# Adding the shift of the rows on one engine, the sigmoid ahead of the rows, and the first row loads on another queue

## The chip, the cores and the metric

The kernel runs on one core of a Trainium2 chip. TensorE (PE), VectorE (DVE), ScalarE (ACT), GpSimd (POOL) and SyncE (SP) each run an instruction stream of their own and meet through semaphores; SP, ACT and POOL can also issue transfers, each on a queue of its own, and 16 DMA engines carry them. The metric is the time of one execution on the device in microseconds (us). Lower is better.

## What is computed

Two layers (DEPTH = 2) over 256 latent tokens and 256 context tokens of width 1024; the second layer processes only the 256 latent tokens. Each layer has a block of token mixers and then a mixture of 16 experts with grouped routing. The part that matters here is the second:

```python
hx2 = modulate(rms_norm(x, g_norm2[l]), sh2, sc2)      # h * (1 + scale) + shift
...
s = jax.nn.sigmoid((t @ w_router).astype(F32))
sel = s + b_router.astype(F32)
grp_score = jnp.sum(lax.top_k(grp, TOP_K)[0], axis=-1)  # best of 4 groups
_, eidx = lax.top_k(jnp.where(emask, sel, -jnp.inf), TOP_K)   # 2 experts inside it
...
for e in range(N_EXPERTS):
    y = (jax.nn.silu(t @ w_gate[e]) * (t @ w_up[e])) @ w_down[e]
    out = out + combine[:, e:e + 1] * y
```

All tensors are float32. The weights of one expert are 6 MB, so each layer reads 96 MB of them.

## The kernel before

**Routing.** When a layer's mixers are done, PE transposes the normalised activations into rows of tokens (`rows`, one bank for each half row of 512 columns of a tile of 128 tokens; four tiles in layer 0, two in layer 1). ACT evicts each half with the token's norm as a factor into `trow` (`rows_out_`, semaphore `row_a`). The modulation's shift is still missing in these rows; it is added to `trow` from `shift_b`, a copy of the shift on all partitions, one for each sequence. The order of the tiles is that of `row_tile`: 2, 3, 0, 1 in layer 0 and 0, 1 in layer 1. POOL adds it to all tiles but tile 1, half by half (L742), DVE to tile 1 (L1234 in the trace, the line of a helper that records every `tensor_tensor`; other helpers' lines are L1237, L1240 and, for ACT, L774).

ACT also takes the sigmoid of the router's logits (`rt`), behind its first two evictions. From it DVE makes the routing in some 40 small instructions (`grp`, `rt`, `tokv`), ending in `routed`; PE makes from its masks the place of each token in its expert (`places`, L2332 to L2334).

**Steps.** Experts are ranked by their number of tokens. An order written out by hand (`ORDER`) runs 27 steps in layer 0 and 18 in layer 1; a step is one expert with up to 64 of its tokens (`C`; some have 32). The experts 0 and 1 (`LEADERS`) come first in both layers, with weights that are loaded ahead. Weights lie in two slots of six units of 1 MB (`wexp`), and SP issues a unit when the step that last used its place has freed it (`used`), in an order fixed by the plan. In a step PE does: gate and up (L2393), the transposes of the next step's rows (L1962), the down product of the step before (L2408), and the turn of this step's result (L1962 or L2442). In layer 1 the weighted results are also added up on PE (`combine`, L2426).

**How rows reach a step.** The first four steps of layer 0 and the first two of layer 1 (`PICKED`) pick their rows from `trow` by a product with a 0/1 matrix `pick` that DVE makes (L2377, `step_rows`). All later steps load theirs from DRAM: POOL writes `trow` with indirect transfers to `x_rows` in the experts' order (`rowid` gives the place; L752, semaphore `scattered`; eight in layer 0, four in layer 1), and the rows of a step are then loaded to `xpick` (four places, `XR`). The first three row loads of a layer are issued by SP (L562) in the midst of its weights, ahead of expert 10 in layer 0 and of expert 6 in layer 1 (`ROWS_AHEAD`), after a wait for `scattered`; the others by ACT (L1086), one for each step. The transposes of a loaded step's rows stand in PE's order ahead of the down product of the step before.

Of the kernel before, what the change touches and what calls it, by code (L numbers as in the profile page):

```python
# [10 lines left out]
ROWS_AHEAD = (10, 6)  # L11
# [149 lines left out]
def hybrid_backbone(nc, A, out):  # L161
# [139 lines left out]
    with ctx:  # L301
# [159 lines left out]
        shift_b = [at_byte("shift_b0", [P, D], f32, CONV), at_byte("shift_b1", [P, D], f32, R6)]  # L461
# [78 lines left out]
        def span(l):  # L540

            return TOK if l < DEPTH - 1 else SEQ

        def seqs(l):
            return span(l) // SEQ

# [13 lines left out]
        def _(sp):  # L560
# [3 lines left out]
            for l in range(DEPTH):  # L564
# [70 lines left out]
                for r, j in plan.issue(plan.loads[LEADERS[l]:], 4, EC):  # L635
                    if (r, j) == (ROWS_AHEAD[l], 0):

                        sp.wait_ge(sem("all", "scattered"), sum(2 * (span(i) // P) for i in range(l + 1)) * 16)
                        for i in range(XR - 1):
                            row, w = plan.steps[PICKED[l] + i][3:]  # L640
                            load(l, f"xload{i}", xpick[0:w, i, :], x_rows[l][row:row + w, :])
# [41 lines left out]
        def _(pool):  # L683
# [5 lines left out]
            for l in range(DEPTH):  # L689
# [43 lines left out]
                NT = T // P  # L733
                pool.wait_ge(sem("all", "x_back2"), back2(l))
                for t in [row_tile(l, b)[0] for b in range(NT)]:
                    if t == 1:
                        continue
                    for c in range(2):
                        b = [row_tile(l, b) for b in range(2 * NT)].index((t, c))
                        pool.wait_ge(S("row_a"), b + 1)  # L740
                        h = slice(c * 512, (c + 1) * 512)
                        ins = nc.gpsimd.tensor_tensor(trow[:, t, h], trow[:, t, h], shift_b[t // 2][:, h], ADD)  # L742
                        if c == 0:
                            p.step(ins)
                    ins.then_inc(S("hm"), 1)
                p.sync()
                pool.wait_ge(S("hm"), 2 * KT + NT - 1)
                pool.wait_ge(S("h2"), seqs(l) * KT + 1)
                pool.wait_ge(S("rowid_ok"), 1)
                for t in range(T // P):  # L750
                    for c in range(2):
# [3 lines left out]
                        ).then_inc(sem("all", "scattered"), 16)  # L755

# [15 lines left out]
        def _(act):  # L772
# [6 lines left out]
            for l in range(DEPTH):  # L779
# [289 lines left out]
                for b in range(2):  # L1069
                    rows_out_(b)  # L1070
                act.wait_ge(S("lgT"), 3)
                fn(rt[:, 0, 0:NT * NE], rt[:, 0, 0:NT * NE], ACT.Sigmoid).then_inc(S("affin"), 1)
                for b in range(2, 2 * NT):
                    rows_out_(b)
# [112 lines left out]
                def scale_first(t):  # L1187

                    act.wait_ge(sem("all", f"yg{t}"), (l + 1) * 2 * 16)
# [39 lines left out]
        def _(dve):  # L1229
# [15 lines left out]
            for l in range(DEPTH):  # L1245
# [461 lines left out]
                for c in range(2):  # L1707
# [4 lines left out]
                    if c == 0:  # L1712
                        v.step(ins)
# [863 lines left out]
```

## Time and profile before

| | us |
|---|---|
| median of 3 runs | 1424.6 |
| lowest, highest | 1423.45, 1424.93 |
| the profiled execution, its own time | 1430.6 |
| its span | 1428.8 |
| PE busy | 1252.2 (88%) |
| DVE busy | 627.1 (44%) |
| ACT busy | 366.2 (26%) |
| POOL busy | 131.5 (9%) |

The rows come from one profiled execution. Its page cuts the span into 40 slices of 35.7 us and gives each engine's busy share in tenths. Other views give single instructions in order of time, with the idle time ahead of them and who ended it, or the busy time of all engines in a chosen stretch. A float32 product appears as two PE instructions.

### The profile page before, as it was taken

The numbers are of one execution on the slowest core, as the hardware profiler recorded it, in microseconds if no ns is written. First come the engines' busy times: TensorE is split into PE (matmuls) and PEld (weight loads), VectorE is DVE, ScalarE is ACT, GpSimd is POOL, SyncE is SP. The second block draws the span as 40 slices with busy tenths as digits, with TensorE's granted clock in tenths as the row PEclk, the third lists the DMA queues.
The fourth block names the chain that finished last, engine by engine and source line by source line (L and its number), as shares of the span: only waits on it lengthen the run. The fifth ranks groups of instructions, "written<-read, shape, count | busy, mean of one in ns | idle before, by whom it ended". The sixth has DMA issues, their size and how long they took to land.

```text
span 1428.8 us, 20033 instructions
## 1 busy us (share of the span) xinstructions
PE 1252.2 (88%) x8172; PEld 794.8 (56%) x8172; DVE 627.1 (44%) x1124; ACT 366.2 (26%) x595; POOL 131.5 (9%) x121
## 2 busy tenths in 40 slices
PE   3699897899999787999999957987899978898986
PEld 1477576787787632334343326775789843343443
DVE  2627448685546442122131126575776661221222
ACT  2632125334243300000100014523454520000000
POOL 0000000000004220000000020004940210000000
PEclk9899999999999989999999987998999989999998
DMA  9747894232224469699899983866264579999996
GB/s 382 283 187 318 362 395 165 89 89 89 89 89 151 198 260 349 249 360 349 330 353 398 415 325 116 324 265 220 105 136 161 193 291 363 389 395 399 396 420 267
DMA packets 59887, 382.71 MB, mean 268 GB/s; under 512 B 8913, under 2 KB 11413, under 8 KB 20309
## 3 DMA queue, kind: packets, MB, share of 16 engines
q1 hardware_dynamic: 45968, 346.18, 62.5%
q10 hardware_dynamic: 9748, 18.74, 4.0%
q0 software_dynamic: 4080, 16.53, 3.2%
q8 instruction: 64, 1.05, 0.3%
q14 instruction: 27, 0.21, 0.0%
HBM read 363.84 MB, written 44.84 MB: 286 GB/s over the span
## 4 chain that ended last, share of the span: by engine, by line
issue 24%; PE 22%; DMA 9%; DVE 7%; ACT 2%; POOL 2%; SPq 0%; POOLq 0%; DVEq 0%; ACTq 0%
DMA wexp<-in_expert 7%; PE bank L2408 3%; PE bank L1995 3%; PE bank L1996 3%; PE bank L1997 3%; PE bank L2393 3%; PE bank L1962 2%; PE bank L2426 1%; DMA x_rows<-trow,rowid 1%; DVE wlo L1234 1%; POOL x_rows L752 1%; DVE rt L1234 1%; DMA stage<-in_in 1%; POOL m_lo L721 1%; PE bank L2274 1%
## 5 line engine op out<-in xcount | busy, mean ns | idle before, releaser
L2393 PE MATMUL bank<-wexp,xg 128*64 128x512 f32 (+1 forms) x1504 | 265.5, 596 | 12.0 <-DMA wexp<-in_expert 9.0
L1995 PE MATMUL bank<-h_hi,whi 128*128 128x512 f32 (+1 forms) x640 | 226.1, 353 | 23.0 <-DVE wlo L1234 13.8
L1996 PE MATMUL bank<-h_lo,whi 128*128 128x512 f32 (+1 forms) x640 | 220.5, 345 | 0.0
L1997 PE MATMUL bank<-h_hi,wlo 128*128 128x512 f32 (+1 forms) x640 | 220.3, 344 | 0.0
L2393 PEld LDWEIGHTS bank<-wexp,xg 128*64 128x64 f32 (+1 forms) x1504 | 77.8, 125 | 164.2 <-issue 144.7
L2408 PE MATMUL bank<-wexp,act_a 128*32 128x256 f32 (+1 forms) x1072 | 151.9, 504 | 16.9 <-DMA wexp<-in_expert 13.9
L1234 DVE TENSOR_TENSOR wlo<-stage,whi 128x2048 fp32r<-128x2048 f32 x56 | 133.3, 2387 | 68.8 <-ACT whi L774 67.1
L1995 PEld LDWEIGHTS bank<-h_hi,whi 128*128 128x128 f32 x640 | 125.1, 195 | 47.8 <-DVE wlo L1234 18.7
L774 ACT ACTIVATE whi<-stage 128x2048 fp32r<-128x2048 f32 x56 | 106.9, 1910 | 101.2 <-DMA stage<-in_in 59.6
L1996 PEld LDWEIGHTS bank<-h_lo,whi 128*128 128x128 f32 x640 | 124.7, 195 | 13.6 <-issue 0.5
L1997 PEld LDWEIGHTS bank<-h_hi,wlo 128*128 128x128 f32 x640 | 124.4, 194 | 13.8
L1234 DVE TENSOR_TENSOR act_a<-act_s,bank 128x256 f32<-128x256 f32 (+1 forms) x47 | 17.1, 364 | 254.8 <-ACT act_s L774 254.8
L774 ACT ACTIVATE yrow<-bank 128x512 f32<-128x512 f32 (+1 forms) x40 | 20.7, 517 | 348.7 <-PE bank L2408 273.4
L1839 DVE COPY gu_sb<-bank 128x512 f32<-128x512 f32 x47 | 32.5, 691 | 166.7 <-PE bank L2393 166.6
L2408 PEld LDWEIGHTS bank<-wexp,act_a 128*32 128x32 f32 (+1 forms) x1072 | 51.0, 129 | 89.8 <-issue 68.5
L1240 DVE SCALAR_TENSOR_TENSOR conv<-glu,vec,conv 128x512 f32<-128x512 f32 (+1 forms) x90 | 57.5, 679 | 1.0 <-DVE amp L1234 0.3
L1962 PEld LDWEIGHTS bank<-tables,xpick 32*128 32x128 f32 (+1 forms) x328 | 24.1, 142 | 46.2 <-issue 31.4
L1995 PE MATMUL bank<-m_hi,whi 128*128 128x512 f32 (+1 forms) x128 | 44.3, 346 | 4.2 <-POOL m_lo L721 4.1
L1996 PE MATMUL bank<-m_lo,whi 128*128 128x512 f32 (+1 forms) x128 | 43.8, 342 | 0.0
L1997 PE MATMUL bank<-m_hi,wlo 128*128 128x512 f32 (+1 forms) x128 | 43.7, 341 | 0.0
L1240 DVE SCALAR_TENSOR_TENSOR xT<-bank,modT,xT 128x256 f32<-128x256 f32 (+1 forms) x64 | 22.7, 409 | 45.4 <-PE bank L1997 38.0
L721 POOL TENSOR_TENSOR m_lo<-merged,m_hi 128x512 fp32r<-128x512 f32 (+1 forms) x16 | 24.1, 1539 | 194.1 <-ACT m_hi L774 194.1
(340 smaller groups left out, 1641.2 us busy)
## 6 DMA issues: line engine op xcount, KB each, us to landing
wexp<-in_expert SPq DMA_DIRECT2D x192, 1024.0 KB, 15.4
stage<-in_in SPq DMA_DIRECT2D x40, 1024.0 KB, 8.5
raw<-in_mod SPq DMA_DIRECT2D x18, 1024.0 KB, 8.2
stage<-in_mod SPq DMA_DIRECT2D x16, 1024.0 KB, 5.0
x_rows<-in_c_zero SPq DMA_DIRECT2D x32, 512.0 KB, 11.1
y_rows<-in_c_zero SPq DMA_DIRECT2D x20, 512.0 KB, 12.0
spare<-in_mod SPq DMA_DIRECT2D x8, 1024.0 KB, 13.7
stage<-in_out SPq DMA_DIRECT2D x8, 1024.0 KB, 4.7
```

Of the source, the lines that this page charges most:

```text
L721: nc.gpsimd.tensor_tensor(m_lo[:, t, 0:T], merged[:, t, 0:T], m_hi[:, t, 0:T].bitcast(f32), SUB).then_inc(S("m_lo"), 1)
L752: pool.indirect_dma_start(out=x_rows[l], out_offset=bass.IndirectOffsetOnAxis(ap=rowid[:, 2 * t + c:2 * t + c + 1], axis=0), in_=trow[:, t ...
L774: return nc.scalar.activation(out_, in_, f, **kw)
L1234: return V.tensor_tensor(o, x, y, op)
L1240: return V.scalar_tensor_tensor(out=o, in0=x, scalar=s, in1=y, op0=op0, op1=op1)
L1839: V.tensor_copy(gu_sb[:, :], bank[0][:, :]).then_inc(S("gu_sb"), 1)
L1962: return nc.tensor.transpose(o, i, ident[0:n, 0:n])
L1995: MM(o, w[0], x_[0], start=start, stop=False)
L1996: MM(o, w[0], x_[1], start=False, stop=False)
L1997: return MM(o, w[1], x_[0], start=False, stop=stop)
L2393: ins = MM(bank[0][g * w:(g + 1) * w, :], x_[:, 2 * j + k, :], wexp[:, z, j, c], start=(first_ == 0), stop=(last_ == 0))
L2408: ins = MM(bank[3][h * w:(h + 1) * w, 0:8 * w], a_[:, kk, :], wexp[:, z, 4 + j, c], start=(kk == 0), stop=(kk == 3))
```

## The change

The shift is added by DVE alone, a whole tile of 1024 columns at a time: the first tile once the routing is done, the others behind the picks of the leading experts. PE's first picked step takes the tiles in the order in which they come and waits for each. POOL's additions and their waits go, and `shift_b1` moves to another place in memory. ACT takes the sigmoid before any eviction. The first three row loads of both layers are issued by POOL, right behind its scatter, and SP no longer waits for the scatter. The semaphores of the rows are counted accordingly.

```diff
-ROWS_AHEAD = (10, 6)
...
-        shift_b = [at_byte("shift_b0", [P, D], f32, CONV), at_byte("shift_b1", [P, D], f32, R6)]
+        shift_b = [at_byte("shift_b0", [P, D], f32, CONV), at_byte("shift_b1", [P, D], f32, RK)]
...
+        def row_loads(r):
+
+            return (r // XR + (1 if r % XR == XR - 1 else 0)) * 16
...
                 for r, j in plan.issue(plan.loads[LEADERS[l]:], 4, EC):
-                    if (r, j) == (ROWS_AHEAD[l], 0):
-
-                        sp.wait_ge(sem("all", "scattered"), sum(2 * (span(i) // P) for i in range(l + 1)) * 16)
-                        for i in range(XR - 1):
-                            row, w = plan.steps[PICKED[l] + i][3:]
-                            load(l, f"xload{i}", xpick[0:w, i, :], x_rows[l][row:row + w, :])
...
-                NT = T // P
-                pool.wait_ge(sem("all", "x_back2"), back2(l))
-                for t in [row_tile(l, b)[0] for b in range(NT)]:
-                    if t == 1:
-                        continue
-                    for c in range(2):
-                        b = [row_tile(l, b) for b in range(2 * NT)].index((t, c))
-                        pool.wait_ge(S("row_a"), b + 1)
-                        h = slice(c * 512, (c + 1) * 512)
-                        ins = nc.gpsimd.tensor_tensor(trow[:, t, h], trow[:, t, h], shift_b[t // 2][:, h], ADD)
-                        if c == 0:
-                            p.step(ins)
-                    ins.then_inc(S("hm"), 1)
-                p.sync()
-                pool.wait_ge(S("hm"), 2 * KT + NT - 1)
-                pool.wait_ge(S("h2"), seqs(l) * KT + 1)
+                pool.wait_ge(S("h2"), seqs(l) * KT + T // P)
                 pool.wait_ge(S("rowid_ok"), 1)
...
+                pool.wait_ge(sem("all", "scattered"), sum(2 * (span(i) // P) for i in range(l + 1)) * 16)
+                for i in range(XR - 1):
+                    row, w = plans[l].steps[PICKED[l] + i][3:]
+                    load("all", f"yg{i}", xpick[0:w, i, :], x_rows[l][row:row + w, :])
...
                 act.wait_ge(S("hn"), (KT if l == 0 else 2 * KT) + 1)
-                for b in range(2):
-                    rows_out_(b)
                 act.wait_ge(S("lgT"), 3)
                 fn(rt[:, 0, 0:NT * NE], rt[:, 0, 0:NT * NE], ACT.Sigmoid).then_inc(S("affin"), 1)
-                for b in range(2, 2 * NT):
+                for b in range(2 * NT):
                     rows_out_(b)
...
                 ins.then_inc(S("routed"), 1)
-                for c in range(2):
-
-                    dve.wait_ge(S("row_a"), [row_tile(l, b) for b in range(2 * NT)].index((1, c)) + 1)
-                    h = slice(c * 512, (c + 1) * 512)
-                    ins = tt(trow[:, 1, h], trow[:, 1, h], shift_b[0][:, h], ADD)
-                    if c == 0:
-                        v.step(ins)
-                ins.then_inc(S("h2"), 1)
-                v.sync()
-                if NS == 2:
-
-                    dve.wait_ge(S("hm"), 2 * KT + NT // 2)
+                def shift_rows_of(i):
+
+                    b = NT + i
+                    t = row_tile(l, b)[0]
+                    dve.wait_ge(S("row_a"), b + 1)
+                    tt(trow[:, t, :], trow[:, t, :], shift_b[t * P // SEQ][:, :], ADD).then_inc(S("h2"), 1)
+
+                shift_rows_of(0)
                 dve.wait_ge(S("places"), 1)
...
+                for i in range(1, NT):
+                    shift_rows_of(i)
+                dve.wait_ge(S("h2"), NS * KT + NT)
...
-                pe.wait_ge(S("hm"), 2 * KT + NT - 1)
-                pe.wait_ge(S("h2"), NS * KT + 1)
...
                     if r >= 0:
-                        pe.wait_ge(S(f"xload{r % XR}"), (r // XR + 1) * 16)
+                        if r < XR - 1:
+                            pe.wait_ge(sem("all", f"yg{r}"), l * 48 + 16)
+                        else:
+                            pe.wait_ge(S(f"xload{r % XR}"), row_loads(r))
...
-                    for t in range(NT):
+                    for i in range(NT):
+                        t = row_tile(l, NT + i)[0]
+                        if s == 0:
+                            pe.wait_ge(S("h2"), NS * KT + i + 1)
                         for g in range(n):
-                            ins = MM(picked_rows(s)[1][g * w:(g + 1) * w, 0:dn], pick[:, s % 3, t * w:(t + 1) * w], trow[:, t, g * dn:(g + 1) * dn], start=(t == 0), stop=(t == NT - 1))
+                            ins = MM(picked_rows(s)[1][g * w:(g + 1) * w, 0:dn], pick[:, s % 3, t * w:(t + 1) * w], trow[:, t, g * dn:(g + 1) * dn], start=(i == 0), stop=(i == NT - 1))
```

## Rows read from the trace of the kernel before

**Rows 1.** The page's slices: busy tenths of PE and of the DMA engines.
```profile
PE   3699897899999787999999957987899978898986
...
DMA  9747894232224469699899983866264579999996
```

**Rows 2.** Timeline, layer 0's routing: start, length, engine, line, operation [idle before <- who ended it].
```profile
488.62 1.48 ACT L774 ACTIVATE trow<-bank,small 128x512 f32<-128x512 f32 x2 [0.15 <-PE bank L1962]
...
490.34 0.48 DVE L1234 TENSOR_TENSOR rt<-rt,router_b 128x64 f32<-128x64 f32 x1 [2.12 <-ACT rt L774]
490.86 0.48 DVE L1234 TENSOR_TENSOR grp<-rt 128x16 f32<-128x16 f32 x4
...
492.46 6.13 POOL L742 TENSOR_TENSOR trow<-trow,shift_b 128x512 f32<-128x512 f32 x5 [1.72 <-ACT trow L774]
...
493.79 0.17 DVE L1684 TENSOR_REDUCE tokv<-grp 128x4 f32<-128x16 f32 x1
...
496.23 2.45 DVE L1234 TENSOR_TENSOR rt<-rt,grp 128x64 f32<-128x64 f32 x2
...
502.67 1.28 DVE L1234 TENSOR_TENSOR trow<-trow,shift_b 128x512 f32<-128x512 f32 x2
...
505.76 9.90 PE L2377 MATMUL bank<-trow,pick 128*64 128x512 f32 x32 [1.49 <-DVE pick L1234]
```

**Rows 3.** Two stretches of layer 0's routing: us, busy us of each engine (instructions), clock, DMA.
```profile
492.40:498.70 6.30, 0.44 (x5) 0.20 (x2) 6.07 (x7) 3.00 (x4) 6.13 (x5) 0.93 1.01 427
498.70:501.80 3.10, 0.00 (x0) 0.00 (x0) 2.68 (x12) 0.00 (x0) 0.00 (x0) 0.50 1.01 423
```

**Rows 4.** Timeline of PE around the first loaded step of layer 0.
```profile
551.64 3.65 PE L2408 MATMUL bank<-wexp,act_a 128*64 128x512 f32 x16
...
570.37 1.06 PE L1962 MATMUL bank<-tables,xpick 32*128 32x32 f32 x8 [7.47 <-DMA xpick<-x_rows]
571.36 6.09 PE L2408 MATMUL bank<-wexp,act_a 128*64 128x512 f32 x16
```

**Rows 5.** By tile, layer 0: the last scatter of POOL, then SP's three row loads.
```profile
L752 POOL DMA_INDIRECT x_rows<-trow,rowid x1: 963/963/963, 525.1 to 525.1; - x1
...
DMA to landing us min/median/max: 21.6/21.6/21.6
...
L562 SPq DMA_DIRECT2D xpick<-x_rows x3: 429/522/578, 555.8 to 556.9; - x3
...
DMA to landing us min/median/max: 14.5/14.7/14.9
```

**Rows 6.** DMA issues: queue, count, KB each, median us to landing.
```profile
xpick<-x_rows ACTq DMA_DIRECT2D x19, 128.0 KB, 6.9
```

**Rows 7.** Timeline, layer 1: two evictions, start of the routing, first row loads, first loaded step.
```profile
1152.74 1.26 ACT L774 ACTIVATE trow<-bank,small 128x512 f32<-128x512 f32 x2
...
1154.22 0.66 DVE L1234 TENSOR_TENSOR rt<-rt,router_b 128x32 f32<-128x32 f32 x1 [2.15 <-ACT rt L774]
1154.92 1.42 DVE L1234 TENSOR_TENSOR grp<-rt 128x8 f32<-128x8 f32 x4
...
1192.91 1.83 SPq L562 DMA_DIRECT2D xpick<-x_rows  x3
...
1195.59 1.06 PE L1962 MATMUL bank<-tables,xpick 32*128 32x32 f32 x8 [5.59 <-DMA xpick<-x_rows]
```

**Rows 8.** Three stretches of layer 1, with the columns of rows 3.
```profile
1172.00:1178.00 6.00, 5.71 (x28) 2.00 (x30) 4.14 (x18) 0.24 (x1) 2.81 (x3) 1.00 0.42 123
1191.00:1195.50 4.50, 0.00 (x0) 0.00 (x0) 1.02 (x2) 0.38 (x1) 0.00 (x0) 0.85 0.53 164
...
1208.30:1411.00 202.70, 181.13 (x1408) 80.81 (x1404) 45.18 (x102) 13.40 (x33) 0.00 (x0) 0.96 1.01 401
```

**Rows 9.** By tile, layer 1: the unit of expert 9 that waits for the down product.
```profile
L614 SPq DMA_DIRECT2D wexp<-in_expert x1: 333/333/333, 1200.5 to 1200.5; - x1
...
DMA to landing us min/median/max: 12.5/12.5/12.5
```

More of the change, by code:

```diff
@@ L1187, in scale_first @@
                 def scale_first(t):
-                    act.wait_ge(sem("all", f"yg{t}"), (l + 1) * 2 * 16)
+                    act.wait_ge(sem("all", f"yg{t}"), (l + 1) * 2 * 16 + (16 if t < XR - 1 else 0))
                     if t >= 2:
@@ L2510, in _ @@
                     s = i + STEPS
-                    pe.wait_ge(S(f"xload{LAST % XR}"), (i + LAST // XR + 1) * 16)
+                    pe.wait_ge(S(f"xload{LAST % XR}"), row_loads(LAST) + i * 16)
                     pe.sem_inc(sem("all", "passed"), 1)
```

## The prediction

> **What bounds the kernel now.** I read the page's slices first [rows 1]. PE is busy nearly everywhere, but the change touches two short places: the routing in front of each layer's experts (late in slices 14 and 33) and the first expert steps behind it. PE's line dips there, to 7, 8 and 7 in slices 14 to 16 and to 7 in slice 33; and in the second layer's experts (slices 34 to 39) the DMA line stands at 9 throughout while PE's changes between 8 and 9. So layer 0's experts are bound by PE and layer 1's by the stream of expert weights, and the same edit must be priced differently in the two.
>
> Next the timeline of ACT, DVE, POOL and PE through layer 0's routing [rows 2]. The reader is to see the order of the handovers: ACT evicts two row halves (1.48 us), only then takes the sigmoid; DVE starts the routing at 490.34, released by that sigmoid; POOL adds the shift from 492.46 on; DVE adds its own two halves at 502.67 beside PE's three small products; the picks follow, and PE's first row product starts at 505.76, released by a pick. It is DVE's chain that ends last before 505.76.
>
> Then the same engine in two neighbouring stretches [rows 3]: while POOL works, seven DVE instructions take 6.07 us; right after it, twelve of the same kind take 2.68 us (0.22 each). The exception inside the slow stretch is the reduction of one operand at 0.17 us, while two two-operand ones take 2.45 us [rows 2].
>
> Then PE's timeline through layer 0's first steps [rows 4]: it stands still for 7.47 us before 570.37, waiting for the first row load of `xpick`, so from 562.9; and the 16 products after the stall take 6.09 us where the same 16 took 3.65. The products behind the stall ran at the half clock, the ones before it at the full one. The row loads were issued by SP at 555.8, and landed 14.5 to 14.9 us later; the scatter they depend on had been on POOL's queue since 525.1 and landed at 525.1 + 21.6 = 546.7 [rows 5]. So 9 us passed in which the rows lay ready and SP stood at earlier weight waits, and 14.5 behind the weights in SP's own queue.
>
> Last, layer 1 [rows 7, 8, 9]: SP stops at the scatter until 1192.91, so no weights are issued; the DMA engines are busy 0.42 of 1172 to 1178 and 0.53 of 1191 to 1195.5, i.e. idle 3.5 and 2.1 us. From 1208.3 on they are full (1.01) for 203 us. What counts in layer 1 is therefore when the weights' stream gets going, not when PE does.
>
> **The change, part by part.**
>
> *Sigmoid first.* It goes ahead of the two evictions that held it up, 1.48 us in layer 0 [rows 2], where it could even start before the first eviction did: 1.5 us earlier. In layer 1 the two take 1.26 us [rows 7], which overlap the sigmoid by about 0.1: 1.15 us. The evictions end some 0.2 us later, well before the picks that read them.
>
> *POOL's additions go.* I read the slow DVE stretch as sharing with POOL: 6.07 − 7 × 0.22 = 4.5 us in layer 0, and 0.48 − 0.23 = 0.25 for the first instruction, which lies beside POOL's first addition. Together 4.8. In layer 1 the first takes 0.66 and the four after it 1.42 [rows 7]; undisturbed, one takes 0.22 [rows 3] and the same four in layer 0, before POOL's long run, took 0.48 [rows 2], so 1.4 us.
>
> *DVE's additions come.* One of 1024 columns is costed as the two of 512 that took 1.28 us together [rows 2]; a saved start-up of some 0.1 us is left out. The first lies where the old pair lay, beside PE's products: nothing. The others (three in layer 0, one in layer 1) stand behind the quick picks, where DVE is on nobody's path for PE's first product: PE needs tiles one by one at the half clock, two products a tile of nearly 0.8 us each (eight took 6.09 at mostly that clock [rows 4]), so 1.5 to 1.7 against 1.28 us for DVE. Their cover is that half clock. But behind them on DVE wait the ranking, `rowid` and the later picks, and so POOL's scatter: 3 × 1.28 = 3.84 us later relative to the picks in layer 0, 1.28 in layer 1.
>
> So PE's first row product comes 1.5 + 4.8 = **6.3 us** earlier in layer 0, the scatter 6.3 − 3.8 = 2.5 us earlier. In layer 1 PE comes 1.15 + 1.4 = 2.5 us earlier and the scatter 2.5 − 1.3 = 1.25 us. The removed PE waits on the shift had ended before 504 and cost nothing; `shift_b1`'s new place frees DVE of a wait that had ended too.
>
> *Row loads on POOL, layer 0.* The scatter now lands at 546.7 − 2.5 = 544.2. POOL issues the first load behind it, 1.0 us as one of its indirect ones [rows 5]: 545.2. POOL has nothing else to do until the gathers at the layer's end. PE arrives at 562.9 − 6.3 = 556.6, so a landing time up to 11.4 us is hidden. The landing of a POOL row load isn't in the trace. From below: SP's, with the queues empty, went from 1192.91 to 1195.59, 2.7 us [rows 7]. From above: SP's 14.5 behind weights in the same queue, and 21.6 for the last of eight scatters. Nearest is the row load on another queue than the weights' while these run: ACT's of 128 KB, median 6.9 us [rows 6]. I take 6.9: landed at 552.1, the stall of **7.5 us** is gone, and with it the half clock behind it: 6.09 − 3.65 = 2.4 and 0.4 for the eight transposes, **2.8 us**. Afterwards the steps free their buffers relative to PE, as before, so layer 0 keeps 6.3 + 7.5 + 2.8 = **16.6 us**.
>
> The Trainium skill speaks against this part: "DMA: Bandwidth & Descriptors", Issuing engine by pattern, puts simple loads on Sync and calls that path generally faster than GpSimd's. The same page, Anatomy of one DMA, fits a GpSimd DMA at 2.0 us plus its bytes at 436 GB/s: by that this load would land in 2.3 us, an estimate, so layer 0 would gain the same and layer 1 its cap of 4.6 us (below), and the sum would be larger by 0.6. No row of before shows such a load under traffic.
>
> *Row loads on POOL, layer 1.* SP no longer stops, so the next four units follow as PE's second step frees them, and the 2.1 us of idle close; 2.5 of the 3.5 us before close as PE is earlier. 4.6 us is what can be had there. But units four and five of expert 9 wait for the down product, which PE does only after the transposes of the first loaded rows. Scatter landed 1192.9 − 1.25 = 1191.7, load issued 1192.7, landed + 6.9 = 1199.6, transposes 1.06, half of the down product at the low clock 3.0 (of 6.09 [rows 4]): 1203.7. Then that unit alone: 1.05 MB at 401 GB/s, 2.6 us [rows 8], and 2.7 of latency by SP's row load: 1209.0. Before it was issued at 1200.5 and landed 12.5 us later, at 1213.0 [rows 9]. Gain 4.0 us; a landing of 2.7 would reach the other cap, 4.6. PE restarts 4 us later than before, but it waited for weights later in the layer anyway. I take **4 us**.
>
> **Sum.** 16.6 + 4.0 = 20.6 us. The profiled execution took 1430.6 us (its span 1428.8); 1430.6 − 20.6 = 1410.0. That execution lies 6.0 us above the median of the runs, 1424.6, so I predict 1424.6 − 20.6 = **1404**.
>
> **Rivals.** Write L for the landing time of POOL's row loads.
>
> *Forecast*, L of 3 to 11: 1404, own range 1401 to 1407. Chance 0.50.
>
> *The clock stays at 2.4 GHz (more gain).* PE's rest before the picks, nearly 10 us [rows 3], shrinks to some 4. If the clock doesn't fall, layer 0's first picks are bound by DVE's 1.28 a tile instead of 1.7 (1.3 us), and layer 1 reaches its cap with denser traffic, 5.6: 23.5 us, 1401. For it, PE's rest would end about where the granted clock was still 0.93; against it, that clock was 0.50 right after [rows 3], so it had fallen within those 10 us, and where exactly can move. Chance 0.13.
>
> *Layer 1 gives nothing*: freed of SP's stop, the weights crowd the scatter, so that rows come some 4 us later still. 16.6 alone: 1408. For it, in layer 0, with weights running, the last scatter took 21.6 us against 14.4 by the same reckoning in layer 1 (1178.5 to 1192.9); against, it was the last of eight there and of four here. Chance 0.15.
>
> *POOL isn't what slows DVE* (the change does not do what it says): the 4.8 and 1.4 stay. Layer 0: 1.5 + 7.5 + 2.8 = 11.8, as L = 6.9 is still covered; layer 1 4.0 − 1.4 = 2.6: 1410. Against it, the slow stretch ends with POOL's last addition to 0.1 us. Chance 0.05.
>
> *Row loads as slow as SP's were*, L = 14.5. Layer 0 then stalls 14.5 − 11.4 = 3.1 and may lose the clock again: 6.3 + 4.4 + (0 to 2.8); layer 1: the unit lands at 1209.0 + 7.6 = 1216.6, a loss of 3.6. Together 7 to 10: about 1416. For it, 14.5 was measured at just this place; against, that queue had weights ahead and POOL's has none. Chance 0.10.
>
> *Slower*: POOL's queue starves beside the weights, L = 21.6 as the last scatter. Gains are 6.3 + 7.5 − (L − 11.4) in layer 0 and about 11 − L in layer 1, so 36 − 2L: it decides from L = 18. At 21.6 it is 7 us slower, 1432. Chance 0.07, of which 0.02 falls on no change.
>
> A measurement of this kernel tells about 0.2% (3 us) from none. Faster 0.93, same 0.02, slower 0.05. The range leaves out the last two cases: from 1398 (the larger gain, and a shorter DVE addition) to 1413 (POOL not the cause, and L near 11).
>
> **What would show it.** Right: in layer 0 the seven DVE instructions near 0.2 us; sigmoid before the first eviction; PE's first row product some 6 us earlier in the stretch, the wait before the step-4 transposes gone and the 16 products behind them at 3.65 us; in layer 1 no SP wait for the scatter, row loads of POOL landing in 3 to 11 us, PE idle about 10 us before the first loaded rows, DMA above 0.9 from 1172 on except a dip of some 2 us. Wrong: a wait of PE for `xpick` behind POOL's loads in layer 0; PE waiting for DVE's additions in the picks; a longer wait in layer 1 that shifts the weights' stream back; or later stretches of layer 0 in which PE, being earlier, waits for weights, which would take back part of the 16.6.

## The result, and the profile after

The changed kernel takes 1412.5 us (median of nine runs, 1406.2 to 1416.7), the kernel before 1424.0 beside it (nine runs, 1418.6 to 1427.6). The medians differ by 11.5 us, where the sum said 20.6; the ratio is 0.9917, with a 95% interval of 0.9897 to 0.9936, which makes 11.8 us. The time lies 8.5 us above the point, outside the forecast's own range of 1401 to 1407, and 0.5 us inside the wide one, 1398 to 1413. The direction was right, the size was not. One assumption of the sum, used in both layers, is why.

The page of the changed kernel: span, then slices of PE and of the DMA engines.

```profile
span 1414.7 us, 20021 instructions
...
PE   3699897899999898999989956997999985998996
...
DMA  9747994242224389999899982865254488999996
```

PE's dip to 7, 8 and 7 in slices 14 to 16 [rows 1] is now 8, 9 and 8. In layer 1 slice 33 went from 7 to 8, but slice 34 from 8 to 5: that is where to look.

To compare the two executions by layer I count from ACT's table load ahead of each layer's sigmoid: 487.18 and 1151.44 before, 486.01 and 1137.11 after. What lies ahead of the first is 1.2 us of drift, and no part of the change. Layer 0 and the mixers behind it gained (1151.44 − 487.18) − (1137.11 − 486.01) = 13.2 us (16.6 forecast); layer 1, from its table load to the end of the span, 14.1 − 14.3 = −0.2 (4.0 forecast).

Layer 0's routing after, in the timeline (start, length, engine, line, operation).

```profile
487.30 0.26 ACT L761 ACTIVATE rt<-rt 128x64 f32<-128x64 f32 x1
487.46 2.60 ACT L761 ACTIVATE trow<-bank,small 128x512 f32<-128x512 f32 x4
487.66 0.22 DVE L1219 TENSOR_TENSOR rt<-rt,router_b 128x64 f32<-128x64 f32 x1 [0.62 <-ACT rt L761]
...
490.48 0.48 DVE L1219 TENSOR_TENSOR rt<-rt,grp 128x64 f32<-128x64 f32 x2
...
494.95 1.22 DVE L1219 TENSOR_TENSOR trow<-trow,shift_b 128x1024 f32<-128x1024 f32 x1
...
497.86 1.12 PE L2365 MATMUL bank<-trow,pick 128*64 128x512 f32 x2 [1.30 <-DVE pick L1219]
```

The sigmoid stands ahead of the evictions, the pair that took 2.45 us [rows 2] takes 0.48, and one addition of 1024 columns takes 1.22. PE's first row product starts at 497.86 instead of 505.76, 6.7 us earlier from the table load. The 32 products take 8.44 us instead of 9.90, another 1.5. The granted clock did fall to 0.50, but it was back at 500.6, 2.8 us after the first of these products, where it had come back at 511.5, 5.7 us after it.

PE around the first loaded step, then by tile the last scatter and POOL's first row load.

```profile
557.15 0.68 PE L1946 MATMUL bank<-tables,xpick 32*128 32x32 f32 x8 [3.62 <-DMA xpick<-x_rows]
557.76 5.35 PE L2396 MATMUL bank<-wexp,act_a 128*64 128x512 f32 x16
```
```profile
L734 POOL DMA_INDIRECT x_rows<-trow,rowid x1: 961/961/961, 520.9 to 520.9; - x1
...
DMA to landing us min/median/max: 28.0/28.0/28.0
```
```profile
L684 POOL DMA_DIRECT2D xpick<-x_rows x1: 554/554/554, 549.2 to 549.2; - x1
...
DMA to landing us min/median/max: 7.9/7.9/7.9
```

The wait for `xpick` is halved, 7.47 to 3.62 us, not gone [rows 4]. The row load itself took 7.9 us against 6.9 assumed; the scatter ahead of it took 28.0 from its last issue, where it had taken 21.6 [rows 5], and so landed at 548.9, later than the 546.7 before although issued 4.3 us sooner.

Layer 1 in the timeline, and three stretches of it (us, busy us of PE, PEld, DVE, ACT, POOL with instructions, clock, DMA share, GB/s).

```profile
1162.21 0.96 POOL L734 DMA_INDIRECT x_rows<-trow,rowid  x1 [0.30 <-issue]
...
1179.94 1.63 POOL L684 DMA_DIRECT2D xpick<-x_rows  x3 [16.77 <-DMA x_rows<-trow,rowid]
1187.07 1.05 PE L1946 MATMUL bank<-tables,xpick 32*128 32x32 f32 x8 [14.71 <-DMA xpick<-x_rows]
1188.05 6.35 PE L2396 MATMUL bank<-wexp,act_a 128*64 128x512 f32 x16
```
```profile
1186.00:1190.00 4.00, 2.93 (x14) 1.64 (x16) 0.42 (x1) 0.00 (x0) 0.00 (x0) 0.50 0.78 142
1190.00:1194.00 4.00, 4.00 (x14) 1.00 (x10) 0.00 (x0) 0.00 (x0) 0.00 (x0) 0.56 0.20 49
...
1200.00:1397.00 197.00, 182.47 (x1410) 81.56 (x1406) 45.27 (x102) 13.40 (x33) 0.00 (x0) 0.96 1.01 400
```

SP's stop is gone, yet PE waits 14.71 us for the rows (5.59 before [rows 7]), and the DMA engines run dry while PE does the down product at the half clock. Idle before: 3.5 + 2.1 = 5.6 us [rows 8]. Idle after: 0.9 and 3.2 in these two stretches and 0.7 in 1161 to 1172.4 (share 0.94), 4.8 together. The hole moved; it hardly closed.

### The profile page after: what moved, and what is told of

It is laid out like the page before. It is cut to its first block, busy times and chain, and to the rows that moved or that the text cites. A ratio compares the mean times of both kernels' runs of the same rounds, so it can differ in the third digit from the quotient of the medians.

```text
span 1414.7 us, 20021 instructions
## 1 busy us (share of the span) xinstructions
PE 1252.0 (88%) x8172; PEld 795.5 (56%) x8172; DVE 625.9 (44%) x1126; ACT 366.0 (26%) x595; POOL 124.4 (9%) x119
## 4 chain that ended last, share of the span: by engine, by line
PE 23%; issue 22%; DMA 10%; DVE 7%; ACT 2%; POOL 2%; SPq 0%; DVEq 0%; POOLq 0%; ACTq 0%
DMA wexp<-in_expert 5%; PE bank L2381 4%; PE bank L2396 4%; DMA x_rows<-trow,rowid 3%; PE bank L1979 3%; PE bank L1980 3%; PE bank L1981 3%; PE bank L1946 2%; PE bank L2414 1%; DVE wlo L1219 1%; DMA stage<-in_in 1%; POOL x_rows L734 1%; POOL m_lo L718 1%; PE bank L2258 1%; PE bank L2071 1%
## 5 line engine op out<-in xcount | busy, mean ns | idle before, releaser
L1979 PE MATMUL bank<-h_hi,whi 128*128 128x512 f32 (+1 forms) x640 | 227.3, 355 | 23.7 <-DVE wlo L1219 14.5
L2396 PE MATMUL bank<-wexp,act_a 128*32 128x256 f32 (+1 forms) x1072 | 151.5, 508 | 11.2 <-DMA wexp<-in_expert 8.1
L1219 DVE TENSOR_TENSOR act_a<-act_s,bank 128x256 f32<-128x256 f32 (+1 forms) x47 | 17.1, 365 | 259.4 <-ACT act_s L761 259.4
L1946 PEld LDWEIGHTS bank<-tables,xpick 32*128 32x128 f32 (+1 forms) x328 | 24.3, 143 | 52.3 <-issue 32.2
L1946 PE MATMUL bank<-tables,xpick 32*128 32x32 f32 (+1 forms) x328 | 29.4, 231 | 18.3 <-DMA xpick<-x_rows 18.3
## 6 DMA issues: line engine op xcount, KB each, us to landing
spare<-in_mod SPq DMA_DIRECT2D x8, 1024.0 KB, 13.7
```

Of the source, the lines that this page charges most:

```text
L1219: return V.tensor_tensor(o, x, y, op)
L1946: return nc.tensor.transpose(o, i, ident[0:n, 0:n])
L1979: MM(o, w[0], x_[0], start=start, stop=False)
L2396: ins = MM(bank[3][h * w:(h + 1) * w, 0:8 * w], a_[:, kk, :], wexp[:, z, 4 + j, c], start=(kk == 0), stop=(kk == 3))
```

## Experiments

Twelve experiments follow; down_l1_again is down_l1 once more. The gains are of each one's profiled execution against the profiled one of before, counted from the table loads: "steps" up to DVE's `act_a` of the last of layer 0's 27 steps, "layer 0" up to the next table load, which takes in layer 1's mixers, and "layer 1" from there to the end of the span. The ratio is that of the runs to those of before beside them. "Scatter" is the time in layer 0 from the last scatter's issue to the first row load, which starts some 0.3 us after it lands (on SP: when SP gets there).

| kernel | us | ratio [95%] | steps | layer 0 | layer 1 | scatter |
|---|---|---|---|---|---|---|
| the change | 1412.5 | 0.9917 [0.9897, 0.9936] | 12.9 | 13.2 | −0.2 | 28.3 |
| rows_on_sp | 1415.9 | 0.9917 [0.9887, 0.9948] | 9.9 | 13.4 | 0.3 | 28.6 |
| rows_only | 1417.9 | 0.9941 [0.9922, 0.9961] | 6.7 | 5.9 | 0.0 | 24.6 |
| sp_stop_l1 | 1411.2 | 0.9887 [0.9858, 0.9916] | 13.0 | 13.1 | 2.6 | 28.3 |
| down_first | 1411.2 | 0.9894 [0.9871, 0.9918] | 10.4 | 12.9 | 7.6 | 28.9 |
| down_l1 | 1405.5 | 0.9855 [0.9829, 0.9880] | 11.0 | 16.0 | 3.7 | 27.7 |
| down_l1_again | 1412.6 | 0.9904 [0.9877, 0.9932] | 12.3 | 13.1 | 3.3 | 28.5 |
| hold_l0 | 1411.9 | 0.9912 [0.9893, 0.9931] | 6.8 | 12.0 | 7.5 | 19.5 |
| two_out | 1410.1 | 0.9898 [0.9876, 0.9919] | 18.2 | 19.7 | −0.1 | 25.4 |
| two_out_down | 1407.8 | 0.9895 [0.9864, 0.9926] | 18.1 | 19.5 | 5.6 | 25.7 |
| two_out_hold | 1406.7 | 0.9873 [0.9846, 0.9900] | 16.3 | 17.1 | 4.2 | 19.1 |
| pool_busy | 1424.6 | one run | 6.2 | 9.3 | −3.5 | 27.7 |
| sigmoid_only | 1426.3 | one run | 2.8 | 3.4 | 2.5 | |

The ends of the "steps" column, before and after:

```profile
825.56 0.29 DVE L1234 TENSOR_TENSOR act_a<-act_s,bank 128x128 f32<-128x128 f32 x1 [5.74 <-ACT act_s L774]
```
```profile
811.53 0.29 DVE L1219 TENSOR_TENSOR act_a<-act_s,bank 128x128 f32<-128x128 f32 x1 [5.80 <-ACT act_s L761]
```

How far each column can be trusted follows from stretches in which kernels have the same code. Layer 1 is the same in the six executions with the down product first, and they read 3.3 to 7.6 there. Layer 0 is the same in the change, sp_stop_l1 and both executions of down_l1: 11.0 to 13.0 in the steps, but 13.1 to 16.0 up to the next table load. Of down_l1's 16.0 us 5.0 came up only behind the steps, where these kernels have the same code. So I read effects in layer 0 from the steps, take 2 us there as noise, and 4 us in the last two gain columns, unless a wait in the timeline stands behind a difference.

**rows_on_sp: the routing's part alone.** The changed kernel, with the row loads given back to SP.

```diff
                 for r, j in plan.issue(plan.loads[LEADERS[l]:], 4, EC):
+                    if (r, j) == (ROWS_AHEAD[l], 0):
+                        sp.wait_ge(sem("all", "scattered"), ...)
+                        for i in range(XR - 1):
+                            load(l, f"xload{i}", xpick[0:w, i, :], x_rows[l][row:row + w, :])
```

> The changed kernel with one part undone: the first three row loads are issued by SP again, in the midst of its weights, after its wait for the scatter. DVE's additions and the early sigmoid stay. Theory (the weights crowd the scatter, and POOL's loads themselves are quick): in layer 0 SP reaches the row loads about 9 us earlier than before, they land 14 to 15 us later behind weights, PE waits 7 to 8 us for them as before; layer 0 keeps only the earlier start, 8 us. In layer 1 SP's stop keeps weights off the scatter, whose last transfer lands about 14.4 us after its issue instead of 17.4; that layer gains 1 to 3 us over before. Together 9 to 11 us faster than before. Rival (the row loads on POOL gave nothing in sum): the same time as the changed kernel, 11 to 14 us below before, with a layer 1 that is some 5 us better and a layer 0 that is 5 us worse.

In layer 0 SP reached its row loads at 548.68, and they landed 9.8 us later, not 14.5 [rows 5]. In the timeline of rows_on_sp:

```profile
558.51 1.06 PE L1948 MATMUL bank<-tables,xpick 32*128 32x32 f32 x8 [5.73 <-DMA xpick<-x_rows]
```

With everything else equal, POOL's loads brought PE its rows 1.6 us earlier, counted from the table load, and the transposes and products behind them ran 1.2 us shorter (1.06 + 6.22 against 0.68 + 5.35): 2.8 us at step 4. It lasts through the steps (9.9 against 12.9), and is gone at the next table load (13.4 and 13.2) only because this execution gained another 3.5 us on before's behind the steps, where it has the changed kernel's code and that one gained 0.3. So POOL's loads are worth some 3 us in layer 0. In layer 1 SP's stop kept the weights off: the scatter was in at 1175.5, and SP's rows landed 2.9 us after their issue. The runs are 10.4 us faster than those of before beside them, within the 9 to 11 expected; the ratio is that of the whole change, and its interval doesn't exclude 3 us either way.

**rows_only: the row loads' part alone.** The kernel before, with the loads moved to POOL (the `+` lines of `row_loads` and of POOL's block in the diff of the change).

> The kernel before with one part alone: the first three row loads are issued by POOL behind its scatter and SP doesn't wait for it; POOL's additions and the late sigmoid stay. Theory: in layer 0 the scatter lands near 546.7 as before, the first row load some 8 us after its issue, near 556, before PE asks at 562.9: the 7.5 us stall and the half clock behind it are gone, 10 us. In layer 1 the scatter lands 17 us after its issue instead of 14.4 and PE restarts 5 to 8 us later; the stream of weights resumes where it did, gain 0. Total 10 us faster than before. Rival (the crowding came only from PE being earlier against a scatter that was not): layer 1's scatter still lands at 14.4 and the layer gains 4 us, total 14.

PE did not wait for rows at all in layer 0 (transposes at 563.52, without idle time), yet this is worth only 5.9 us there (6.7 in the steps), not the 10 expected: at the next step PE waits for `act_a`. In the timeline of rows_only:

```profile
571.55 0.60 ACT L777 ACTIVATE yrow<-bank 128x512 f32<-128x512 f32 x1 [13.23 <-DMA y_rows<-yrow]
...
574.33 5.35 PE L2414 MATMUL bank<-wexp,act_a 128*64 128x512 f32 x16 [1.75 <-DVE act_a L1237]
```

This is the first sign of a second limit in layer 0: ACT may not evict a step's output into `yrow` before the write of the one before has landed, and `silu` stands behind that eviction. The parts don't add: 6.7 us from the rows alone and 9.9 from the routing alone in the steps, but 12.9 together (0.59%, 0.83% and 0.83% by the ratios, whose intervals don't exclude the sum for certain). The timelines name the reason: both feed the same wait. The expectations of the scatter missed: in layer 0 it landed some 24.3 us after its last issue instead of 21.6, and in layer 1 after some 15.0, between the theory's 17 and the rival's 14.4.

**sp_stop_l1: do the weights crowd layer 1's scatter?** The changed kernel; SP waits for the scatter in layer 1 before unit (6, 0).

```diff
+                    if l == DEPTH - 1 and (r, j) == (6, 0):
+                        sp.wait_ge(sem("all", "scattered"), ...)
```

> The changed kernel with SP's wait for the scatter put back in layer 1, ahead of the first unit of expert 6; the row loads stay on POOL. Theory (crowding by the weights that SP issues during the scatter): the last scatter lands 14 to 15 us after its issue instead of 17.4, POOL's first row load 3 to 4 us after its issue instead of 7.1, and PE restarts 6 us earlier than in the changed kernel; the DMA engines idle 2 to 3 us while SP waits. The unit that waits for the down product lands 2 us earlier; total 1 to 3 us faster than the changed kernel. Rival (the scatter is slow by itself): it still takes 17 us, SP's units come 12 us later and the kernel is 3 or more us slower than the changed one.

Its timeline in layer 1, and POOL's first row load by tile:

```profile
1162.12 0.96 POOL L736 DMA_INDIRECT x_rows<-trow,rowid  x1 [0.30 <-issue]
...
1176.02 1.63 POOL L686 DMA_DIRECT2D xpick<-x_rows  x3 [12.93 <-DMA x_rows<-trow,rowid]
1178.84 1.06 PE L1948 MATMUL bank<-tables,xpick 32*128 32x32 f32 x8 [6.57 <-DMA xpick<-x_rows]
```
```profile
DMA to landing us min/median/max: 2.8/2.8/2.8
```

With the weights held back the scatter took 3.7 us less (13.7 from the last issue), the row load 2.8 us instead of 7.1, and PE got its rows 8.2 us earlier. Layer 1 gained 2.6 in place of −0.2, which by itself would be within the noise. Crowding is shown by the two landings, for the scatter and for the row load. The Trainium skill ("DMA: Bandwidth & Descriptors", Queues, rings and completion order) says that each DMA engine takes turns between the queues that have work for it, a packet at a time; the traces agree in that both transfers are slower when SP's queue is full. The estimate of 2.3 us for this load by the Trainium skill's fit (same page, Anatomy of one DMA) is near the 2.8 here, and far from the 7.1 to 7.9 beside the weights.

**down_first and down_l1: put work into the wait.** PE does the down product, which needs no new rows, before the transposes of the first loaded rows; down_first in both layers, down_l1 in layer 1 alone.

```diff
-                    if s + 1 < STEPS:
+                    if s + 1 < STEPS and not (l == DEPTH - 1 and s == PICKED[l] - 1):
                         step_columns(s + 1)
...
                         down(*step(s - 1))
+                    if l == DEPTH - 1 and s == PICKED[l] - 1:
+                        step_columns(s + 1)
```

> The changed kernel with PE's order changed at one step of each layer: the down product of the step before comes ahead of the transposes of the first loaded rows, and in layer 1 ACT waits for the scatter one step later so that this product can be fed. Theory (what costs in both layers is that PE's down product, and with it two units of weights, stand behind the late rows): in layer 0 the 3.6 us wait shrinks to near 0 and the product runs at the full clock, 4 to 5 us; in layer 1 the two units of expert 9 are issued some 15 us earlier, the DMA engines don't run dry (share 0.9 or more where it was 0.20), 3 to 5 us. Together 7 to 10 us faster than the changed kernel. Rival (the units crowd the rows): the rows land 3 to 6 us later still, PE waits longer for them, and layer 1 gains nothing: 4 us in all.

> The changed kernel with the down product ahead of the first loaded rows' transposes in layer 1 alone, and ACT's wait for the scatter one step later there. Theory (in layer 1 the dry DMA engines are the cost, in layer 0 PE's order was fine): layer 0 as in the changed kernel, 13 us over before; layer 1 7 us over before instead of 0, since two units are issued some 15 us earlier and DMA never falls below 0.9. In all 18 to 21 us faster than before, ratio 0.986 to 0.988. Rival (the gain of layer 1 in the run of both was drift between executions): the same as the changed kernel, 0.991 to 0.992.

Stretches of layer 1 in down_l1, with the columns of before:

```profile
1186.00:1190.00 4.00, 4.00 (x23) 1.85 (x26) 2.06 (x5) 0.38 (x1) 0.00 (x0) 0.50 1.02 277
1190.00:1194.00 4.00, 4.00 (x34) 1.31 (x28) 0.59 (x1) 0.00 (x0) 0.00 (x0) 0.77 1.01 338
```

The hole of the DMA engines at 1186 to 1194 is gone: the unit behind the down product goes out ahead of the rows. All five versions with this order gain 3.3 to 7.6 us in layer 1, the four that have POOL's loads without it and without a stop 0.0 or less (0.0 in rows_only, −0.1, −0.2, and −3.5 in pool_busy, where the scatter was issued 2.7 us later in its layer than in the change). In layer 0 the same order costs: at 557.69 PE waited 2.84 us for `act_a` in down_first, since there the rows are nearly in and ACT's chain is not; the steps give 10.4 us where the change has 12.9. So down_first's 0.9894 is 3 us below the change's ratio, not the 7 to 10 expected. down_l1's 0.9855 is even below the 0.986 to 0.988 of its theory, but with 3.7 us in layer 1 in place of 7, and it did not come again (see down_l1_again).

**hold_l0: the same crowding in layer 0.** down_l1, and SP waits for layer 0's scatter before unit (9, 2).

```diff
+                    if l == 0 and (r, j) == (9, 2):
+                        sp.wait_ge(sem("all", "scattered"), 2 * (span(0) // P) * 16)
```

> The same, and in layer 0 SP waits for the whole scatter ahead of the third unit of expert 9, so that fewer weights share the DMA engines with it. Theory (crowding): the last scatter of layer 0 lands 22 to 25 us after its issue instead of 28.0, the first row load some 4 us after its issue instead of 7.9, and PE's wait of 3.6 us and the half clock behind it shrink to at most 1 us: 4 to 5 us faster than the run without the hold. Rival (the scatter is slow by its own number of transfers, 3.6 us each): it lands as late, the held weights come later and PE waits for them one step on: the same or 3 us slower.

The scatter landed 19.2 us after its last issue, at 541.4, and PE had its rows without waiting. But in its timeline of layer 0:

```profile
559.91 3.38 PE L2398 MATMUL bank<-wexp,act_a 128*64 128x512 f32 x8 [1.95 <-DMA wexp<-in_expert]
...
569.64 0.60 ACT L763 ACTIVATE yrow<-bank 128x512 f32<-128x512 f32 x1 [19.61 <-DMA y_rows<-yrow]
```

The held weights come late, and the write of `yrow`, issued at 548.4, landed at 569.6. So the crowding of layer 0 is shown, and also that rows in time don't pay by themselves: the steps give 6.8 us, 4.2 to 5.5 less than in down_l1, and what makes it 12.0 in the next column came behind the steps. The 4 to 5 us expected from the hold were not there.

**pool_busy: is it POOL that slows DVE?** The changed kernel, with POOL doing as many additions of 512 columns as before, on `shift_b` alone and into a scratch buffer that nobody reads; ACT's first eviction of picked rows, which reuses that buffer's place, waits for them.

```diff
+                        ins = nc.gpsimd.tensor_tensor(scratch[:, :], shift_b[0][:, h], shift_b[0][:, h], ADD)
```

> The changed kernel, and POOL also does additions that nobody uses (128x512, two operands, six in layer 0 and two in layer 1, one after another behind ACT's evictions, into a free place). Theory (DVE was slowed by sharing with POOL): DVE's small two-operand instructions that lie beside these take 1.0 to 1.2 us each again instead of 0.2, reductions stay at 0.2, and PE's first picked product comes 3 to 5 us later than in the changed kernel. Rival (the slow stretch had another cause): DVE stays at 0.2 us each and nothing moves.

Its timeline in layer 0's routing:

```profile
492.78 0.18 DVE L1237 TENSOR_SCALAR grp<-grp 128x16 f32<-128x16 f32 x1
492.90 2.16 POOL L740 TENSOR_TENSOR scratch<-shift_b 128x512 f32<-128x512 f32 x2 [0.18 <-POOL scratch L740]
492.99 2.14 DVE L1234 TENSOR_TENSOR rt<-rt,grp 128x64 f32<-128x64 f32 x2
...
495.17 0.22 DVE L1679 TENSOR_REDUCE tokv<-rt 128x4 f32<-128x64 f32 x1
...
495.42 0.93 DVE L1234 TENSOR_TENSOR rt<-rt,tokv 128x64 f32<-128x64 f32 x1
```

The pair is slow again, 2.14 us, and PE's first row product comes 4.9 us later than in the changed kernel, counted from the table load. Nothing depends on POOL's result, so it is the sharing, not the data. POOL's additions take 1.04 us each, and each of the slow DVE instructions with two SBUF inputs ends within 0.1 us after one of them; the reduction between them, with one input, takes its usual 0.22. The Trainium skill has this rule ("GPSIMD Engine Reference", Specifications: the SBUF interfaces are shared with VectorE, with contention for instructions in a 2-port perf mode or with two SBUF inputs), and the trace agrees for two inputs. The number of inputs is not the whole of it: in the trace of before a `TENSOR_SCALAR`, for which the row names one tensor, took 1.19 us beside POOL, against 0.18 in the changed kernel. Whether the rule's other half covers it no run here shows.

```profile
495.01 1.19 DVE L1237 TENSOR_SCALAR grp<-grp 128x16 f32<-128x16 f32 x1
```

**sigmoid_only: the order of ACT alone.** The kernel before, with the sigmoid ahead of the first two evictions.

> The kernel before with the sigmoid ahead of ACT's evictions as its only edit. Theory: DVE starts the routing 1.5 us earlier in layer 0 but meets POOL's additions as before and for longer; PE's first picked product comes 1 to 1.5 us earlier in layer 0, 1 us in layer 1; in all 1 to 3 us, within the drift between executions. Rival (the order of ACT was not what held DVE): nothing moves.

DVE started earlier, but met more of POOL's additions: PE's first row product came only 0.8 us earlier, from the table load, than before. The 1.5 us are worth their size only once POOL is out of the way.

**two_out, two_out_down, two_out_hold: the second limit of layer 0.** A second output buffer for steps 1, 3 and 5 of layer 0, in the changed kernel, in down_l1 and in hold_l0; and down_l1 once more.

```diff
-                    fn(yrow[:, 0:w * 8], bank[3][:, 0:w * 8], ACT.Copy).then_inc(S("y_ev"), 1)
+                    odd = isinstance(s, int) and s in (1, 3, 5)
+                    buf = yrow_b if odd else yrow
+                    fn(buf[:, 0:w * 8], bank[3][:, 0:w * 8], ACT.Copy).then_inc(S("y_ev"), 1)
```

> The changed kernel with a second buffer (yrow_b) for the outputs of steps 1, 3 and 5 of layer 0, so that ACT's eviction of a step's output doesn't wait for the write of the one before to land. Theory (a second limit lies right behind the late rows: the one output buffer, whose write takes 9 to 13 us to land in layer 0; in the changed kernel it is hidden by the wait for the rows): ACT's idle of 9.27 us before the eviction at 564.3 no longer ends at the write but at PE's product, and the time stays within 2 us of the changed kernel's 1412.5, since PE did not wait there. Rival (the changed kernel's layer 0 is held by that buffer as well): 3 to 5 us faster, 1408 to 1409.

> The version with layer 1's down product ahead of the transposes of the first loaded rows (down_l1, 1405.5), and the second output buffer. In that version's layer 0 the rows came earlier and PE then waited 3.5 us for act_a, behind an eviction that waited for the write of yrow, and ran the 16 products behind it at the half clock (5.35 instead of 3.65). Theory (the output buffer is the next limit): that wait and the slow products go, 3.5 + 1.7 = 5 us, layer 0 ends 5 us earlier and the median is 1400 to 1402. Rival (the next weights or the rows of the following step hold PE then): 1404 to 1406, with a wait of PE for wexp or xpick in its place.

> As two_out_down, and SP stops in layer 0 before weight unit (9, 2) until the scatter has landed (as in hold_l0, 1411.9, where rows were in time but PE waited 1.95 us for weights and 4.1 for act_a). Theory (output buffer): the 4.1 us and the half clock behind it go, 4 to 6 us: 1406 to 1408, still held by the late weights. Rival (the weights held back are what costs, the buffer only the first to show it): the wait moves on to wexp and the time stays at 1411 to 1412.

> A second set of runs of down_l1 beside the other three, on the same chip. Theory: its gain is real, 1405 to 1407. Rival (its 1405.5 was the luck of four runs; its profiled execution was 1411): 1408 to 1411.

What the buffer was to take away stands in the timeline of down_l1's layer 0, ahead of step 5:

```profile
566.73 0.60 ACT L761 ACTIVATE yrow<-bank 128x512 f32<-128x512 f32 x1 [11.41 <-DMA y_rows<-yrow]
...
569.49 5.35 PE L2396 MATMUL bank<-wexp,act_a 128*64 128x512 f32 x16 [3.53 <-DVE act_a L1219]
```

And the same place in two_out:

```profile
554.50 0.68 PE L1955 MATMUL bank<-tables,xpick 32*128 32x32 f32 x8
555.11 3.65 PE L2405 MATMUL bank<-wexp,act_a 128*64 128x512 f32 x16
...
558.81 0.60 ACT L761 ACTIVATE yrow<-bank 128x512 f32<-128x512 f32 x1 [6.51 <-PE bank L2405]
...
563.49 3.65 PE L2405 MATMUL bank<-wexp,act_a 128*64 128x512 f32 x16
```

ACT now waits for PE's product, and the products of the next step run at 3.65 too. The profiled executions of two_out and two_out_down gain 18.2 and 18.1 us in the steps, more than any version without the buffer (at most 13.0). Part of that I had not foreseen and can't explain: their scatter was in 25.4 and 25.7 us after its last issue, against 27.7 to 28.9 in five executions with the changed routing, POOL's loads, one buffer and no hold. So PE's wait for the rows (3.62 us) and the slow products behind it (1.7) were gone in two_out as well, and these two alone make up its 5.3 us over the change; the buffer's part is that nothing took them back.

The clean pair is hold_l0 and two_out_hold, which differ in the buffer alone and whose scatters were in after 19.5 and 19.1 us: 6.8 and 16.3 us in the steps. PE's wait of 4.11 us for `act_a` is gone, and of its waits only those for the held weights are left (0.42 and 1.91 us), as the theory said; the median of 1406.7 lies in its 1406 to 1408. In the medians the buffer's gain is small: two_out stands at 0.9898 against 0.9917 with overlapping intervals, two_out_down 4.8 us below down_l1_again beside it, again with overlapping ranges, and above the 1400 to 1402 expected. And down_l1 itself came out at 0.9855 and then 0.9904, 1.6 us above even the rival's 1408 to 1411, so its first number was partly luck. The versions that add something to the change lie at 0.9855 to 0.9912. That down_l1 beats the change is likely by its two results, but their intervals don't settle it (0.9904's overlaps that of the change), and which version is the best can't be told.

## Why the prediction was right in direction and wrong in size

**Routing: right.** 6.3 us forecast, 6.7 measured. POOL as the cause of DVE's slow stretch is shown by pool_busy. DVE's addition of 1024 columns took 1.22 against 1.28. PE has no idle time for it in the picks; only its weight loads, which run ahead, waited 2.3 us in three places. The clock gave 1.5 more, by coming back sooner. That is the size of the picks' part in the rival in which it stays up (1.3), though it did not stay up.

**The step that failed: "The scatter now lands at 546.7 − 2.5 = 544.2".** Its issue came 3.1 us earlier from the table load, a little better than 2.5. But the 21.6 us to its landing were carried over from before as if they were a property of the scatter. They belong to what shares the DMA engines. The earlier picks brought SP's weights forward by 8.2 us, the scatter by 3.1 alone, so SP's first unit behind the picks went out 11.2 us ahead of the last scatter's issue, where it had been 6.1 (509.7 and 520.9, 519.1 and 525.1), and the landing took 28.0. Two experiments lie in order between these: by the table's last column 24.6 us with the unit 7.2 us ahead (rows_only) and 27.7 with 10.1 (pool_busy), against 28.3. The bytes of the packets in the traces say the same: at the last issue 2.9 MB of the eight scatters had still to be moved before and 3.7 after, and until the landing SP's queue moved 6.1 and 7.8 MB beside them. Both come to about 0.41 MB per us. hold_l0, with 3.3 MB of weights beside the last of the scatter, got the landing down to 19.2. So of the 7.5 us of stall 3.9 were won, of the 2.8 of the clock 1.1 (1.06 + 6.09 to 0.68 + 5.35). The sum for layer 0 closes: 6.7 + 1.5 + 3.9 + 1.1 = 13.2.

**L, POOL's row load: right.** 6.9 assumed, first loads at 7.9 in layer 0 and 7.1 in layer 1. The rivals with L of 14.5 and 21.6 did not happen. It was the transfer in front of this one that slowed down.

**Layer 1: the same step failed, and its rival came true.** "Scatter landed 1192.9 − 1.25" kept 14.4 us; it was 17.4, since SP no longer stopped. With the row load behind it at 7.1, PE's down product and with it the unit of expert 9 came late: issued at 1191.9, landed 4.8 us later at 1196.7, which is 2.0 us earlier from the table load than before's 1213.0 [rows 9], not 4.0. Even that overstates it: the stream had stood dry for 4.1 us in front of this unit, and by the idle sums above (5.6 and 4.8) the layer could gain 0.8. This is the case "the weights crowd the scatter", to which I gave 0.15; it held in layer 1 and, what I had not considered, also in part of layer 0. sp_stop_l1 and the versions with the down product first show both halves of the chain.

**The end of the sum.** The profiled spans differ by 14.1 us, the medians by 11.5. Executions of one kernel lie up to 15 us apart here, so the two agree. That the time fell inside the wide range is luck in part: its upper end stood for POOL not being the cause and for a slow row load, and neither happened. The case that did, priced at 1408 with layer 0's 16.6 us whole, was 4.5 us too fast, mostly since it left layer 0's scatter as it was (13.2 us in place of 16.6). Had the rows come in time, the forecast would still have met the output buffer in layer 0: rows_only and down_l1 lost 1.8 and 3.5 us of PE to it, and 1.7 of clock behind it. The sentence that the steps "free their buffers relative to PE, as before" left out the one buffer that is freed by a landing.

## What to carry to other kernels

A landing time read from the trace holds only with the traffic beside it: when a change moves the start of a large stream relative to a small transfer on the path, price the small one again, between its time on idle engines and its time at the back of full ones. If two edits feed the same wait, what each gives alone can't be added up (6.7 and 9.9 us here, but 12.9 together). And before a wait is booked as gain, look for the next thing due there, buffers freed by a write's landing included; where the wait can't be taken away, put work ahead of it that needs nothing of it, first of all work that lets the next loads out.

## What the runs showed of the hardware

- The last of eight scatters landed 28.0 us after its issue beside a full weight stream, 21.6 with the stream starting 5.1 us later against it, 19.2 with part of it held back. In the first two the bytes moved from the issue to the landing, over that time, give the same 0.41 MB per us.
- A POOL row load landed after 2.8 us with SP's queue stopped, after 7.1 and 7.9 beside it; SP's own after 2.9 with nothing of its queue ahead (rows_on_sp, layer 1), and behind weights after 9.8 in rows_on_sp and 14.5 before.
- POOL's additions slowed DVE's small instructions with two SBUF inputs from 0.22 to 0.9 or 1.1 us each, even with no data in common, and left a reduction in their midst at 0.22; a `TENSOR_SCALAR` of one tensor went from 0.18 to 1.19 as well.
- Behind the waits of PE of 3.5 to 15.7 us in these traces the 16 down products that came next took 5.0 to 6.4 us, against 3.65 at the full clock, so such a wait cost another 1.3 to 2.7 us behind it. Behind shorter ones it went either way: 5.35 behind 1.75 us in rows_only and behind 3.01 in down_first, 3.65 behind 2.84 in down_first and behind 1.64 in down_l1.
